# Front of a one-core inference step: one tile's moments behind the second folding, a smaller feature load, one warming product moved, u's low halves ahead of the last odd-spectrum steps

## The reference

```
sh1, sc1, g1, sh2, sc2, g2 = modulation(c, w_mod, b_mod)      # silu(c) @ w_mod + b_mod
u = layer_norm(x) * (1.0 + sc1) + sh1
z = u @ w_in                                                   # 1024 x 2816
...
h = sin(freq[0] * (feats @ w1 + b1))                           # Hyena filter, feats: L x 33
h = sin(freq[1] * (h @ w2 + b2))
h = (h @ w3) * exp(-t * |decay|)
filt_f = rfft(circular(h))
```

## Time and profile before

| what | value |
|---|---|
| median of 3 runs | 634.61 us (634.25, 636.15, 634.61) |
| the profiled execution: its own time | 633.17 us |
| the profiled execution: span, first to last instruction | 631.3 us |
| mean granted TensorE clock over the span | 0.997 |
| PE busy | 600.8 us, 95% |
| DVE, ACT, POOL busy | 440.5, 305.6, 188.4 us |
| chain that ended last | PE 82%, DVE 7%, DMA 5%, ACT 4% |

### The profile page before, as it was taken

How to read it: one execution, slowest core, us unless ns; L and a number is a source line. 1 busy time by engine, 2 the same in 40 slices (tenths; PEclk the granted TensorE clock), 3 DMA queues, 4 the chain that set the end, 5 groups by cost and what they waited for, 6 DMA issues and landing times.

```text
span 631.3 us, 9327 instructions
## 1 busy us (share of the span) xinstructions
PE 600.8 (95%) x3353; PEld 455.3 (72%) x3353; DVE 440.5 (70%) x757; ACT 305.6 (48%) x506; POOL 188.4 (30%) x152
## 2 busy tenths in 40 slices
PE   6899999999999988998999999989999999999994
PEld 2237999999999965557888888747767677676352
DVE  4967766834994654467553499988998877983187
ACT  2748122335344543005795342846565655752354
POOL 1002333345551307041496070421212221321121
PEclk9999999999999999999999999999999999999998
DMA  9985852222221269764980706769999999999788
GB/s 305 387 305 222 305 186 97 101 101 100 101 68 66 92 238 325 303 264 99 290 271 36 294 8 234 280 168 370 393 376 403 390 388 406 374 364 372 291 299 144
DMA packets 40040, 154.89 MB, mean 245 GB/s; under 512 B 7049, under 2 KB 17033, under 8 KB 27451
## 3 DMA queue, kind: packets, MB, share of 16 engines
q1 hardware_dynamic: 27912, 115.41, 50.6%
q10 hardware_dynamic: 5522, 23.48, 9.4%
q0 software_dynamic: 6560, 15.42, 8.3%
HBM read 141.59 MB, written 23.63 MB: 262 GB/s over the span
## 4 chain that ended last, share of the span: by engine, by line
PE 82%; DVE 7%; DMA 5%; ACT 4%; issue 2%; POOL 0%; DVEq 0%; ACTq 0%; POOLq 0%
PE bank L1898 13%; PE bank L1574 12%; PE bank L1575 12%; PE bank L1770 9%; PE bank L1952 8%; PE bank L1410 3%; PE bank L1747 2%; PE bank L1674 2%; PE bank L1880 2%; DMA arena<-in_w_mod 2%; PE bank L1477 2%; PE bank L1625 2%; PE bank L2011 2%; PE bank L1730 2%; DMA u_scr<-arena 1%
## 5 line engine op out<-in xcount | busy, mean ns | idle before, releaser
L772 POOL TENSOR_TENSOR w_low<-arena,w_high 128x1024 fp32r<-128x1024 f32 x22 | 53.6, 2437 | 145.9 <-ACT w_high L971 145.9
L2544 DVE TENSOR_TENSOR gate_up_low<-arena,gate_up_high 128x1024 fp32r<-128x1024 f32 x64 | 75.3, 1221 | 12.3 <-ACT gate_up_high L1256 10.2
L1256 ACT ACTIVATE gate_up_high<-arena 128x1024 fp32r<-128x1024 f32 x64 | 63.9, 1054 | 15.5 <-DMA arena<-in_moe_w_gu 15.5
L971 ACT ACTIVATE w_high<-arena 128x1024 fp32r<-128x1024 f32 x22 | 23.2, 1058 | 87.8 <-PE bank L1575 87.0
L1574 PE MATMUL bank<-u_high,w_high 128*128 128x320 f32 x176 | 56.3, 320 | 1.7 <-DVE u_low L2157 1.7
L1952 PE MATMUL bank<-arena 128*128 128x512 f32 x128 | 57.7, 593 | 0.0
L1575 PE MATMUL bank<-u_high,w_low 128*128 128x320 f32 x176 | 54.4, 309 | 0.0
L1574 PE MATMUL bank<-u_high,w_low 128*128 128x320 f32 x176 | 54.4, 309 | 0.0
L1574 PE MATMUL bank<-u_low,w_high 128*128 128x320 f32 x176 | 54.4, 309 | 0.0
L1575 PE MATMUL bank<-u_low,w_high 128*128 128x320 f32 x176 | 54.4, 309 | 0.0
L1575 PE MATMUL bank<-u_high,w_high 128*128 128x320 f32 x176 | 54.4, 309 | 0.0
(11 more groups left out here) (442 smaller groups left out, 1396.4 us busy)
## 6 DMA issues: line engine op xcount, KB each, us to landing
arena<-in_moe_w_gu SPq DMA_DIRECT2D x38, 1024.0 KB, 10.1
arena<-in_w_mod SPq DMA_DIRECT2D x24, 1024.0 KB, 6.6
arena<-in_moe_w_down ACTq DMA_DIRECT2D x13, 1024.0 KB
arena<-in_w_in SPq DMA_DIRECT2D x11, 1024.0 KB, 4.8
arena<-in_moe_w_down SPq DMA_DIRECT2D x6, 1024.0 KB
y_scr<-arena SPq DMA_DIRECT2D x11, 512.0 KB, 9.1
arena<-in_x SPq DMA_DIRECT2D x10, 512.0 KB, 9.6
arena<-y_scr SPq DMA_DIRECT2D x10, 512.0 KB, 6.0
```

The costliest lines, as they stand in the source:

```text
L772: G.tensor_tensor(WL[s_][:, :, w], ring[s_][:, :, w], WH[m % 2].bitcast(F), ALU.subtract).then_inc(wl_rdy, 1)
L971: S.activation(WH[m % 2], ring[(m // 2) % 2][:, :, (m % 2) * P:(m % 2 + 1) * P], ACT.Copy).then_inc(wh_rdy, 1)
L1256: S.activation(WGH[j][c], raw_gu[s][:, c, :, :], ACT.Copy).then_inc(wgh_rdy, 1)
L2544: tt_(WGL[s][c], raw_gu[s][:, c, :, :], WGH[j][c].bitcast(F), ALU.subtract).then_inc(wgl_rdy, 1)
```

## The change

- `filt` now holds the features and w1 alone, 33 x 704, and w2 is a load of its own of 128 x 128, issued second on ACT's queue. The first filter layer waits for both (`ld_filt` 32).
- PE: three `front_dense` products in place of four between the two filter layers; one more such product, into bank 0, behind `mod1(1)` and a wait for `eo_win` 1, ahead of the wait for `eo_win` 2.
- DVE: `x_moments(1)` moves from ahead of the second folding to behind it.
- DVE: the last `spectrum_far(3)` and `spectrum_near(3)` each move behind one more `u_low`.

```
@@ build
-        filt = fl.take(NTOK + HIDDEN + P)
-        feats, w1, w2 = filt[:, 0:NTOK], filt[:, NTOK:NTOK + HIDDEN], filt[:, NTOK + HIDDEN:NTOK + HIDDEN + P]
+        filt = fl.take(NTOK + HIDDEN)
+        feats, w1 = filt[:, 0:NTOK], filt[:, NTOK:NTOK + HIDDEN]
+        w2 = fl.take(P)
@@ ScalarE
-            eng.dma_start(filt, t["filt"]).then_inc(ld_filt, 16)
+            eng.dma_start(filt[0:FEATS, :], t["filt"]).then_inc(ld_filt, 16)
+            eng.dma_start(w2, t["hy_w2"]).then_inc(ld_filt, 16)
@@ TensorE
-                    eng.wait_ge(ld_filt, 16)
+                    eng.wait_ge(ld_filt, 32)
...
-            def front_dense(n):
+            def front_dense(n, bank=5):
 
                 for b in range(n):
-                    mm(B[5][:, :], ident, consts[:, 2 * KT:2 * KT + 512], start=True, stop=True)
+                    mm(B[bank][:, :], ident, consts[:, 2 * KT:2 * KT + 512], start=True, stop=True)
 
             front_dense(1)
             filter_layer(0)
-            front_dense(4)
+            front_dense(3)
             filter_layer(1)
...
             mod1(1)
+            eng.wait_ge(eo_win, 1)
+            front_dense(1, 0)
             eng.wait_ge(eo_win, 2)
             filter_rows([(3, 1)], 2)
@@ VectorE
             filter_fold(0)
             x_moments(0)
-            x_moments(1)
             filter_fold(1)
-            for i in range(2, TT):
+            for i in range(1, TT):
                 last = x_moments(i)
...
-                if k == 7:
-                    spectrum_far(3)
             u_low(KT - 2)
+            spectrum_far(3)
+            u_low(KT - 1)
             spectrum_near(3)
-            u_low(KT - 1)
```

More of the change, by code:

```diff
@@ L2909 @@
     pair2[0:HIDDEN, 0:HIDDEN] = pair2[HIDDEN:P, HIDDEN:P] = a["hy_w2"][0]
-    filt = np.zeros((P, NTOK + HIDDEN + P), f32)
-    filt[0:FEATS, 0:NTOK] = features()
-    filt[0:FEATS, NTOK:NTOK + HIDDEN] = a["hy_w1"][0]
-    filt[:, NTOK + HIDDEN:] = pair2
+    filt = np.concatenate([features(), a["hy_w1"][0]], 1).astype(f32)
     rgw = np.zeros((P, 8, P), f32)
@@ L2938 @@
         "brt": np.concatenate([a["router_bg"][0], a["router_be"][0]]),
-        "filt": filt, "hy_w3": a["hy_w3"][0],
+        "filt": filt, "hy_w2": pair2, "hy_w3": a["hy_w3"][0],
         "decay": a["hy_decay"][0].reshape(-1), "dft_taps": spec_tables, "dft": fold_tables,
```

## The result

| | before | changed |
|---|---|---|
| median, 6 runs each | 634.82 us | 631.74 us |
| lowest to highest | 634.19 to 637.58 | 631.33 to 632.39 |
| the profiled execution: time, span | 633.17, 631.3 | 631.71, 629.7 |
| mean granted TensorE clock, profiled | 0.997 | 0.992 |

By the medians the change is 3.1 us faster, where I had said 1.2 against the median shown (634.61), and the measured median lies 0.26 us outside my range. The ratio over the runs is 0.9943, with a 95% interval of 0.9918 to 0.9968; the quotient of the two medians is 0.9951. Between the two profiled executions the distance is only 1.46 us, which is near my sum. Most of the miss sits between the kernel before and its own profile.

The account below looks back on a forecast made before the run. DVE's stream was taken to set the end ahead of 27 us, PE from there on. Terms of -1.46, +0.55 and -0.30 summed to -1.21 us, taking the median 634.61 to 633.4 us, range 632.0 to 635.0.

Parts of the forecast that it names:

- my sum: The whole kernel: -1.46 + 0.55 - 0.30 = -1.21 us.
- Part 1: End of the first projection group: u_low ahead of the last odd spectrum steps on DVE, a gain of 1.46 us.
- The near part: DVE's last near spectrum step, behind u_low7: ends near 63.9 us, 0.4 us before group m = 1 would start.
- Part 3: Opening loads: the smaller filt load lets consts land earlier, a gain of 0.3 us, between 0 and 0.6.
- Part 2: Second folding on DVE: folding earlier, one tile's moments behind it, a loss of 0.55 us.
- late-clock rival: First PE products: clock rises only behind the second layer, Part 2 gains 0.3 us, time 632.6 us; chance 0.10.
- What I cost at nothing: Mainly the product into bank 0: 0.86 us hidden in PE's 1.37 us wait; also w2's extra issue, 0.4 to 0.5 us.
- PE's clock falls in the new gaps: Rival, PE between 18.43 and 27.04 us: half clock in the changed kernel, 638.4 us; chance 0.06.
- swallowed: Rival: the front's 1.2 us vanishes at a later transfer, such as the 8.44 us store; 634.3 us, chance 0.18.
- 27.04: Sign, start of PE's products after the 1.37 us wait: forecast wrong if they come over 0.3 us earlier.
- k = 7: Sign, PE's last step of the first projection group: forecast wrong if it waits over 0.5 us.
- The third: Sign, end of the kernel: forecast wrong if it moves otherwise than the end of k = 7 does.

Follow-up runs that it names:

- e6: The changed kernel without the product into bank 0: 633.99 us, ratio 0.9964 to the kernel before.
- e11: The changed kernel without the product into bank 0, run a second time: 632.86 us, ratio 0.9979 to the kernel before.
- f5: The changed kernel itself, run again on another chip: 632.19 us, ratio 0.9957 to the kernel before.
- e5: The kernel before, unchanged, run again for a second profiled execution: a span of 633.1 us.
- f1: The kernel before, unchanged, a third profiled execution: 635.05 us.
- f2: The kernel before, unchanged, a fourth profiled execution: 634.17 us.
- a1: The changed kernel itself, run again: 633.09 us, ratio 0.9965 to the kernel before.

## Why the prediction was wrong

Forecast were 633.4 us and a range of 632.0 to 635.0; 631.74 came. The step that failed is the product into bank 0, costed at nothing; the load was mis-sized as well.

**Part 1, the reorder: right, to a few hundredths.** I had 1.46 us; the distance from the context spectrum to DVE's read of the first group is 18.11 to 18.17 us in every profile with the new order and 19.55 to 19.67 in every one without. The near part was not late for m = 1.

**Part 3, the load: mis-sized.** My 0.3 us was the middle of 0 and 0.6. In ten profiles with the old load `consts` landed, and PE began, at 4.61 to 4.86 us; in ten with the new one at 3.87 to 4.33 in eight and at 4.69 and 4.72 in two (e6, e11). Against 4.74 the eight are 0.4 to 0.9 us earlier. In mean the twenty profiles give 4.76 with the old load and 4.25 with the new one, a gain of 0.5 us. What failed here is that I let w2 and `decay` take the places of `filt`'s packets. From 2 to 4 us, ACT's queue and SP's queue in the changed kernel moved

```profile
q1 hardware_dynamic: 236, 0.67, 90.5%
q10 hardware_dynamic: 32, 0.05, 8.9%
```

SP's q1 had the engines nearly to itself (0.67 MB). ACT's later loads slipped instead: the absolute value of decay waited until 13.57 in place of 12.52, where it hides. I had also written that the first filter layer won't wait for either load; in f5 it waited 0.2 us for w2.

**Part 2, the moments: the traces bear out the mechanism and, in mean, the price; the runs do not resolve it.** DVE's idle time was 0.89 us for my 0.83 (0.98 and 1.12 in the other two profiles of the changed kernel). From the first product to the first filter part it takes 18.13 us in mean in the eight profiles with the new place and 17.65 in the twelve with the old: a loss of 0.48 for my 0.55, though single executions lie up to 0.7 us off their mean. That the last two passes are always the fast ones was true of one trace only: the second layer of the kernel before began 9.13 us after the first product in the first profile, and 8.46, 8.31 and 9.44 in the others. The rise of the clock moves by a microsecond between executions, both ways, and in those four profiles (the first, e5, f1, f2) DVE idled 0.30, 0, 0 and 0.61 us ahead of the second folding. This is my late-clock rival in a milder form, and it said what the Trainium skill's rule says ("TensorE: Matmul & The Clock Gate", "What's actually happening"): the place of the rise differs from run to run. Here four executions of one program agree with it. The cost that I priced for that rival was not the one that came.

**What I cost at nothing: this step failed.** I wrote that the added product is hidden in the wait of 1.37 us and looked only at what it could cost. It prevents a loss instead. My argument was that this gap was followed by four passes in 1.98 us; in three of eight profiled executions with that gap open it was followed by half clock, which cost 1.59, 1.65 and 3.23 us, 0.8 us when spread over the eight. The granted clocks of the timed runs put it at 1.0 to 1.3. I even had the mechanism among the rivals, as "PE's clock falls in the new gaps", and gave it to the changed kernel as a danger; it was the old kernel's ailment. The new gap ahead of w_mod (0.2 to 2.07 us) did lose the clock in two profiles, of 1.83 us and of 2.07 us of waiting, and cost some 0.6 us in the first, not my 5, since DVE is the bound there.

**How it adds up.** DVE read the first group's result at 65.97, 67.20, 68.69 and 66.41 us in four profiles of the kernel before, mean 67.07, and at 64.84, 64.69 and 65.11 in three of the changed one, mean 64.88: 2.2 us, of which 1.44 are part 1 and 0.75 lie ahead of the context spectrum. These 0.75 are themselves a difference. Bank 0 is written the second time at 26.93 in mean before and at 27.38 in the changed kernel, 0.45 later, and the stretch behind it takes 20.59 before and 19.38 after, 1.2 less. Over all twenty profiles the terms are -1.44 for part 1, -0.51 for the load, +0.48 for the moments and -0.8 for the product: -2.3 us, where my sum was -1.21. The gap between the two sums is the product (0.8) and the load (0.2). The run comparisons say, by ratio, 2.2 (a1), 2.7 (f5) and 3.6 us (the first one), and by medians 2.2, 3.4 and 3.1, with intervals that all hold 2.2. From there to the transposes at 227 us every execution takes 161.4 to 161.5 us, so nothing is swallowed; behind it the rest takes 403.0 to 404.4 us in the four profiles of the kernel before and 402.6 to 403.8 in the three of the changed one. Whatever the first comparison shows beyond the sum is not more than its interval allows; no run here explains it.

**Baseline.** I put the difference to the right median, but derived it from one profile that was the luckiest of four: 633.17 us where later ones read 635.02, 635.05 and 634.17.

**My signs of being wrong.** Two of the three did not come: 27.04 moved to 27.35, and k = 7 waited 0.1 us. The third did: k = 7 and m = 1 moved by 1.18 us and the median by 3.1. What I expected of the first filter part, 0.25 us later, came 0.29 earlier, by the load.

## What to carry to other kernels

A wait of a microsecond on TensorE is not priced by its length alone: the products behind it may run at half clock in some executions and not in others, so a product that nobody reads can be worth more than its time, and one profile of the kernel before can miss this altogether. The mean granted clock of each timed run shows it without a trace. Take several profiled executions before calling a gap harmless, above all where the median lies over the profiled time. Work that a later engine needs goes ahead of work that only frees a bank: that edit, reckoned by the rows, came out to 0.02 us.

## What the hardware showed that I had not expected

- The same program with the same wait of 1.37 us kept or lost the full clock from one execution to the next, in stretches of half clock that cost 1.6 or 3.2 us of PE work. Longer waits did both too: 1.83 and 2.07 us (the changed kernel's first profile, e11) lost it, 1.72 (a1) kept it.
- A load of 33 rows in place of 128 on the other queue let `consts` land up to 0.87 us earlier, more than the 0.6 that the packets' own times gave; but in two of ten profiles with the small load it landed at 4.7 all the same, and no run here tells why.
- Where PE waited for it, the first w_mod block landed at 19.6 to 21.4 us whatever the front did, so a faster front only met it sooner.
